# Both last down products at the end, residual sums in PSUM, and the down bias given once as gates times biases

## The reference

```python
logits = x @ w_router + b_router;  top_v, top_i = top_k(logits, 4);  gates = softmax(top_v)
gate = min(xb @ wg[e] + bg[e], 7);  up = clip(xb @ wu[e] + bu[e], -7, 7)      # 32 experts
y    = ((up + 1) * gate * sigmoid(1.702 * gate)) @ wd[e] + bd[e]
ffn  = sum over a token's 4 experts of its gate * y
out  = layernorm(2**0.25 * x + ffn + sigmoid(x @ w_ple_gate) * (p @ w_ple_proj))
```

## Time and profile before

| | us |
|---|---|
| three executions, median | 1250.95 (1250.07 to 1252.32) |
| profiled execution, its own time | 1253.7 |
| span of its profile | 1251.8 |
| PE busy / DVE / ACT / POOL | 1169.6 / 357.2 / 186.4 / 69.7 |
| moved | 442.18 MB, mean 353 GB/s |

### The profile page before, as it was taken

The page is one execution under the profiler, slowest core; times in us unless marked ns, Lnnn a source line. Parts: engine busy times, 40 slices in busy tenths (PEclk is TensorE's granted clock), DMA queues, the critical chain, the costliest instruction groups (busy, mean ns, idle before and its releaser), DMA issues.

```text
span 1251.8 us, 13175 instructions
## 1 busy us (share of the span) xinstructions
PE 1169.6 (93%) x5601; PEld 485.4 (39%) x5601; DVE 357.2 (29%) x568; ACT 186.4 (15%) x346; POOL 69.7 (6%) x74
## 2 busy tenths in 40 slices
PE   5999999899999997899999999999999999998985
PEld 4678775633333332243333333332323232322221
DVE  6866334531313130111222222122212121213014
ACT  2444342311001010020201000010101010110000
POOL 3100141110101030000000000000000000000000
PEclk9999999699999998999999999999999999999988
DMA  9652130689999999999999999999999999999892
GB/s 313 215 151 68 68 139 19 264 350 380 420 421 421 421 418 386 420 421 422 416 421 420 421 421 421 405 421 421 420 421 421 419 422 413 421 421 421 357 421 86
DMA packets 70509, 442.18 MB, mean 353 GB/s; under 512 B 7952, under 2 KB 8368, under 8 KB 21296
## 3 DMA queue, kind: packets, MB, share of 16 engines
q1 hardware_dynamic: 65600, 425.66, 83.5%
q0 software_dynamic: 4848, 15.64, 3.7%
HBM read 436.54 MB, written 4.73 MB: 353 GB/s over the span
## 4 chain that ended last, share of the span: by engine, by line
PE 73%; DMA 17%; DVE 7%; ACT 2%; issue 1%; SPq 1%; DVEq 0%
PE ps L1011 42%; DMA ring<-in_w_up 12%; PE ps L593 9%; PE ps L992 6%; DMA ring<-in_w_gate 4%; PE ps L944 3%; DVE y_s L1883 3%; PE ps L814 2%; DVE h_s L1881 2%; PE ps L999 2%; PE ps L621 1%; ACT hTe L1162 1%; PE ps L1027 1%; PE ps L976 1%; PE ps L948 1%
## 5 line engine op out<-in xcount | busy, mean ns | idle before, releaser
L1011 PE MATMUL ps<-ring,xTe 128*64 128x512 f32 x1536 | 358.1, 601 | 17.7 <-DMA ring<-in_w_up 14.5
L1011 PEld LDWEIGHTS ps<-ring,xTe 128*64 128x64 f32 x1536 | 105.5, 136 | 242.4 <-issue 242.2
L1011 PE MATMUL ps<-ring,hTe 128*64 128x512 f32 x768 | 180.8, 610 | 7.1 <-DMA ring<-in_w_down 7.1
L1863 DVE TENSOR_TENSOR xs<-xs,ps 128x512 f32<-128x512 f32 x64 | 44.0, 688 | 348.5 <-PE ps L992 348.4
L593 PE MATMUL ps<-xT,ring 128*128 128x288 f32 x448 | 115.4, 414 | 1.0 <-PE ps L593 0.6
L1011 PE MATMUL ps<-more,xTe 128*64 128x512 f32 x496 | 113.5, 599 | 1.6 <-DMA more<-in_w_up 0.8
L1011 PEld LDWEIGHTS ps<-ring,hTe 128*64 128x64 f32 x768 | 52.3, 139 | 121.8 <-issue 121.4
L593 PEld LDWEIGHTS ps<-xT,ring 128*128 128x128 f32 x448 | 84.8, 193 | 25.3 <-issue 2.3
L992 PE MATMUL ps<-y_s,GT 128*128 128x512 f32 (+1 forms) x256 | 82.5, 520 | 2.2 <-ACT y_s L1162 1.2
L1881 DVE TENSOR_SCALAR h_s<-ps 128x512 f32<-128x512 f32 x32 | 21.8, 681 | 161.0 <-PE ps L1011 161.0
L1162 ACT ACTIVATE h_s<-g_s 128x1024 f32<-128x1024 f32 x16 | 16.9, 1056 | 307.7 <-DVE g_s L1871 307.7
(11 more groups left out here) (371 smaller groups left out, 817.8 us busy)
## 6 DMA issues: line engine op xcount, KB each, us to landing
ring<-in_w_gate SPq DMA_DIRECT2D x96, 1024.0 KB, 11.2
ring<-in_w_up SPq DMA_DIRECT2D x96, 1024.0 KB, 11.7
ring<-in_w_down SPq DMA_DIRECT2D x96, 1024.0 KB, 13.6
more<-in_w_gate SPq DMA_DIRECT2D x32, 1024.0 KB, 9.9
more<-in_w_down SPq DMA_DIRECT2D x32, 1024.0 KB, 13.0
more<-in_w_up SPq DMA_DIRECT2D x30, 1024.0 KB, 13.1
ring<-in_w_in SPq DMA_DIRECT2D x28, 512.0 KB, 6.2
ring<-in_w_out SPq DMA_DIRECT2D x8, 512.0 KB, 5.1
```

What stands on the lines that cost most here:

```text
L1011: last = mm(ps[64 * q:64 * q + 64, bank0 + half, :], lhs(k, q), wide(t)[:, k % 2, half * 512:(half + 1) * 512], start=False, stop=k == KT - 1)
L1863: tt(x, x, ps[:, CB_BANKS[n], 0:512 if i < 2 else QW], ALU.add).then_inc(S["cb_added"], 1)
```

## The change

- **Order of the last stages.** gate and up of 14, gate and up of 15, down of 14, down of 15, for SP's loads and TensorE alike. h of 14 is transposed after step 1 of gate(15), h of 15 after step 3 of down(14) into a buffer of its own (`hTe_last`). Shares of pair 14 are made in down(15).
- **Sums in PSUM.** For the last two pairs the residual is brought into five banks by a matmul with the identity, the shares accumulate onto it there, and the statistics and the last norm read the banks. VectorE's adds for pairs 14 and 15 go. y of pair 15 is copied in two halves, by ScalarE and VectorE.
- **Down bias.** The bias matmuls of the down products and the preparation of the third bias vector go. All gates are transposed once, and each unit gets gates times b_down (fp32) in PSUM; b_down is loaded by POOL after the embedding weights.
- **Opening.** The wait for the key transposes moves to the last instruction of tile 1's norm; ScalarE's square root for it stands ahead of its key copies; `select` is split in `top_experts` and `chosen`, and the sample rows' norm comes before the subtractions; `prompt_states_b` runs before the sample rows' transposes; the first gather goes to banks 7 and 2, the gate product starts after the first copy; the second gather moves from up(0) to gate(0).

```diff
@@ tables
+SUM_BANKS = (6, 7, 0, 1, 4)
+LAST = NPAIR - 1
+STAGES = [(p, w) for p in range(NPAIR - 2) for w in range(3)] + \
+         [(LAST - 1, 0), (LAST - 1, 1), (LAST, 0), (LAST, 1), (LAST - 1, 2), (LAST, 2)]
@@ SP
-            for p in range(NPAIR):
-                for t, (w, k, q) in enumerate((w, k, q) for w in range(3) for k in range(KT // 2) for q in range(2)):
-                    t += p * PER
+            for stage, (p, w) in enumerate(STAGES):
+                for t, (k, q) in enumerate((k, q) for k in range(KT // 2) for q in range(2)):
+                    t += stage * KT
@@ POOL
-                for n, name in enumerate(("b_gate", "b_up", "b_down")):
+                for n, name in enumerate(("b_gate", "b_up")):
...
+            pool.wait_ge(S["ple_mm"], 5 * (KT + 1))
+            pool.dma_start(ple_w[0][0:NE, :], a["b_down"][0]).then_inc(S["ple_w_in0"], 16)
@@ TensorE
             row_stats(2)
+            prompt_states_b()
             transpose_normed(2)
...
             sample_ranks()
-            prompt_states_b()
             prompt_states_a()
...
+            def whole_unit(n, whole):
+                return mm(summed(n), ident, unit_of(n), start=True, stop=whole)
+            def all_gates():
+                for i, (t0, r) in enumerate(TILES):
+                    last = nc.tensor.transpose(ps[0:NE, 6, t0:t0 + r], gate_of[0:r, i, 0:NE], ident[0:r, 0:r])
+            def whole_with_bias(n):
+                whole_unit(n, False)
+                i, halves = (n // 2, (n % 2,)) if n < 4 else (2, (0, 1))
+                t0, r = TILES[i]
+                for half in halves:
+                    for out, c in columns(i, half, SUM_BANKS[n]):
+                        mm(out, GT[1][0:NE, t0:t0 + r], ple_w[0][0:NE, c], start=False, stop=False)
+            def last_h(k):
+                if k == 3:
+                    for half in range(2):
+                        h_transposes(LAST, half, half)
+                if k == 5:
+                    pe.wait_ge(S["hTe_ok"], 2 * LAST + 2)
+                if k in (5, 6):
+                    whole_with_bias(k - 3)
@@ products
-                for half in range(2):
+                for half in range(2 if w < 2 else 0):
@@ beside_gate
+                    if k in (1, 3):
+                        if k == 1:
+                            pe.wait_ge(S["OH_ok"], 1)
+                            pe.wait_ge(S["st_ok"], 2)
+                        gather(xTe[0], 2 * (k - 1), 4, 4 + k // 2, 128, 128)
+                    if k == 3:
+                        pe.wait_ge(S["xTe_ok"], 2)
...
+                elif p == LAST:
+                    if k == 1:
+                        for half in range(2):
+                            h_transposes(LAST - 1, half, 4 + half)
+                    if k == 3:
+                        pe.wait_ge(S["cb_added"], 5 * (LAST - 1))
+                        pe.wait_ge(S["ple_added"], 5 * (KT + 1))
+                        all_gates()
@@ beside_up
+                if p == LAST and k in (3, 4):
+                    if k == 3:
+                        pe.wait_ge(S["GT_ok"], NPAIR + 1)
+                        pe.wait_ge(S["ple_w_in0"], 16 * 6)
+                        pe.wait_ge(S["sel_ok"], NPAIR)
+                    whole_with_bias(k - 3)
@@ pairs
-                gather(xTe[0], 4 * n, 4, n, 0, 128)
+                gather(xTe[0], 4 * n, 4, ROW_BANKS[n], 0, 128)
-                pe.wait_ge(S["xTe_ok"], (2, 4)[p] if p < 2 else 4 + 8 * (p // 2))
+                pe.wait_ge(S["xTe_ok"], (1, 4)[p] if p < 2 else 4 + 8 * (p // 2))
...
+            def beside_last_down(k):
+                if 1 <= k <= 5:
+                    if k == 1:
+                        pe.wait_ge(S["y_ok"], LAST)
+                        whole_with_bias(4)
+                    combine_unit(k - 1, GT[(LAST - 1) % 3], SUM_BANKS[k - 1], False, False)
...
+            pe.wait_ge(S["y_ok"], NPAIR + 1)
             for n in range(5):
-                if n >= 2:
-                    pe.wait_ge(S["cb_added"], 5 * (NPAIR - 1) + n - 1)
-                combine_unit(n, GT[(NPAIR - 1) % 3])
+                combine_unit(n, GT[LAST % 3], SUM_BANKS[n], False)
@@ ScalarE
+            copy_y(LAST - 1)
+            act.wait_ge(S["cb_mm"], 5 * LAST)
+            act.wait_ge(S["y_mm"], 4 * LAST + 2)
+            f(y_s[:, 0:512], ps[:, 2, :], ACT.Copy).then_inc(S["y_ok"], 1)
@@ VectorE
+                    if n == 5:
+                        dve.wait_ge(S["kbt_mm"], 1)
...
-            dve.wait_ge(S["kbt_mm"], 1)
             norm(1, 5)
...
-            select(0)
+            top_experts(0)
             mixer_residual(2)
             tile_stats(2)
             spread_stats()
-            rest_of(1, 0)
+            chosen(0)
             norm_stats(2, 6)
             norm_apply(2, 6)
+            rest_of(1, 0)
+            rest_of(2, 0)
             rest_of(1, 1)
...
+            dve.wait_ge(S["cb_mm"], 5 * LAST)
+            dve.wait_ge(S["y_mm"], 4 * LAST + 4)
+            nc.vector.tensor_copy(y_s[:, 512:D], ps[:, 3, :]).then_inc(S["y_ok"], 1)
+            for n in range(5):
+                dve.wait_ge(S["cb_mm"], 5 * NPAIR + n - 4)
+                step(summed_stats(n))
```

More of the change, by code:

```diff
@@ L990, in combine_unit, with products @@
                 for half in halves:
[L991 to L992 removed]
+                    for out, c in columns(i, half, SUM_BANKS[n]):
[8 more added lines that the diff above has]
+                    whole_with_bias(k - 3)
+            def combine_unit(n, gt, bank=None, first=True, last_one=True):
+                bank = CB_BANKS[n] if bank is None else bank
+                i, halves = (n // 2, (n % 2,)) if n < 4 else (2, (0, 1))
+                t0, r = TILES[i]
+                for half in halves:
+                    for out, c in columns(i, half, bank):
+                        last = mm(out, gt[:, t0:t0 + r], y_s[:, c], start=first, stop=last_one)
                 last.then_inc(S["cb_mm"], 1)
[L995 to L998 removed]
+            def products(p, bank0, lhs, w, sel_p, after_k, done):
+                for half in range(2 if w < 2 else 0):
                     mm(ps[:, bank0 + half, :], sel_p[:, :, :].rearrange("p q s -> p (q s)"),
@@ L1001, in products @@
                 for k in range(KT):
-                    tiles = [(p if isinstance(p, int) else NPAIR) * PER + first + 2 * (k // 2) + q for q in range(2)]
+                    first = STAGES.index((p, w)) * KT if isinstance(p, int) else NPAIR * PER + w * KT
+                    tiles = [first + 2 * (k // 2) + q for q in range(2)]
                     if k % 2 == 0:
@@ L1011, in products @@
                             last = mm(ps[64 * q:64 * q + 64, bank0 + half, :], lhs(k, q),
-                                      wide(t)[:, k % 2, half * 512:(half + 1) * 512], start=False, stop=k == KT - 1)
+                                      wide(t)[:, k % 2, half * 512:(half + 1) * 512],
+                                      start=w == 2 and k == 0, stop=k == KT - 1)
                             if k == KT - 1:
@@ L1392, in _ @@
                             f(ple[:, i, 0:w], ple[:, i, 0:w], ACT.Sigmoid).then_inc(S["ple_sig"], 1)
-                else:
+                elif p == 0:
+                    for n in range(2):
+                        copy_rows(2 + n, xTe[0][:, 4 * n:4 * n + 4, 128:256], ps[:, 4 + n, :])
                     for n in range(2):
@@ L1396, in _ @@
                 swish(p)
-                if p == 0:
-                    for n in range(2):
-                        copy_rows(2 + n, xTe[0][:, 4 * n:4 * n + 4, 128:256], ps[:, 4 + n, :])
                 for n in range(4):
@@ L1444, in tile_stats @@
                     last = nc.vector.bn_stats(lns[:, i, q, :], x[:, q * 512:(q + 1) * 512] if i < 2 else x)
-                    (done or step)(last)
+                    step(last)
             def spread_stats():
@@ L2014, in _ @@
                         add_shares(j + NPAIR)
-                dve.wait_ge(S["cb_added"], extra * 5 + 5 * NPAIR)
-                for i in range(3):
-                    tile_stats(i, lambda last: last.then_inc(S["stats_anew"], 1))
+                for n in range(5):
+                    dve.wait_ge(S["out_mm"], 6 + n + 1)
+                    summed_stats(n).then_inc(S["stats_anew"], 1)
                 dve.wait_ge(S["stats_anew"], 5)
```

111 lines of the change are left out of this document (65 added, 46 removed).

## The result

The changed kernel takes 1245.13 us, median of eight executions (1241.68 to 1248.36); the kernel before, run beside it on the same chip, 1252.7 (1250.07 to 1254.13). The profiled execution took 1248.36, its span is 1246.5; it is 5.3 shorter than the span of before and the slowest of the eight.

The account below looks back on a forecast made before the run. The expert stage was taken as bound by the weight stream at about 421 GB/s. Terms 7.5 + 0.6 + 4.9 + 3.05 = 16.05 us, from the median 1250.95, gave 1235 us, range 1229 to 1243.

Parts of the forecast that it names:

- Order of the last stages: Pairs 14 and 15: TensorE goes straight from up(14) to gate(15) and ends 4.9 us earlier.
- 4.8 us loss of the stream: Weight stream near pair 14: 4.8 us lost while down(14) waited for h, to be recovered by the new order.
- TensorE's end: Last two pairs: gate(15) ends at 1167.2, up(15) 1185.6, down(14) 1207.2, down(15) 1226.6, 4.9 us earlier than 1231.5.
- rival 3: TensorE, not the stream, bounds the end, putting it back 2 to 4 us: 1237 to 1239; chance 0.12.
- Opening: Before pair 0: earlier norms, state products off the path and no copy wait bring 7.5 us in all.
- bound on both sides: TensorE's clock in the opening: gain 4.2 us if it returns no earlier, 12 if it never falls.
- rival 4: Stream takes nothing of the opening's gain, lost in a longer stand in pair 0: 1243; chance 0.06.
- Rival 1: Full clock in the opening: 4.5 us more gain, 1230.5; chance 0.15.
- rival 2: Opening gives little, by low-clock gathers or a ScalarE wait: gain 4.2 or less, 1238 to 1240; chance 0.17.
- Rival 5: Slower: opening keeps TensorE at 1.2 GHz through the gathers and into pair 0: 1256; chance 0.02.
- After the last product: From TensorE's end to the statistics' spread: gain 3.05 us; from spread to end unchanged at 11.2 us.
- Down bias: Removing thirty-two bias matmuls: nothing in the bound middle, 0.6 us in pair 0; VectorE's third bias vector: nothing.

Follow-up runs that it names:

- two pairs of runs: The changed kernel and the one with pair 15's selector made before h of pair 14, each run twice: 1245.13 and 1245.35 against 1242.5 and 1240.8 us.
- selector-early: Changed kernel with pair 15's selector made on VectorE before h of pair 14: 1242.5 and 1240.8 us, ratios 0.9915 and 0.9894 to the kernel before.
- fillers: selector-early plus eight 256-column matmuls in the opening whose result nobody reads: 1240.12 us, ratio 0.9903 to the kernel before.
- states in gate(0): selector-early with fillers and the mLSTM state products moved behind step 1 of gate(0): 1241.1 us, ratio 0.9906 to the kernel before.
- selector in the middle: Changed kernel with pair 15's selector made between h of pair 14 and the embedding adds: 1242.03 us, ratio 0.9917 to the kernel before.
- changed again: The changed kernel run a second time, unaltered: 1245.35 us, ratio 0.9935 to the kernel before.

## Why the prediction was wrong, point by point

**Order of the last stages: the step that failed.** I wrote that "after up(14) TensorE goes straight to gate(15)". I had followed h, the tiles and the transposes to their new places, but not the other operand of the product that was moved forward: its selector, made by VectorE at the end of pair 14. No list of waits of before could show this wait, since down(14) covered it; the program could, and so could VectorE's timeline, where `sel` starts at 1156.49, 5.5 us behind the end of up(14). The stand measured 5.87 us. Priced by the two pairs of runs, it cost 4.6 to 4.9 us at the end, and it kept the 4.8 us loss of the stream that I had counted as recovered: by the two stretches from 1140 it was 5.8 us. With the selector early 0.7 is left of it. The prediction's own sign, no stand over 1 us between up(14) and gate(15), failed; the wait that it named as a sign of being wrong, between gate(15) and up(15), stands one product later and did not come.

**TensorE's end: mis-sized by 3.2 us.** With the wait away, level to copy is 117.5, and I had 114.4. Measured from the end of up(14), selector-early takes 16.2 us for gate(15), as forecast; 20.6 for up(15) where I had 18.4, since two waits for tiles of 1.47 in all came already there, the units cost 2.1 each in place of 1.9, and the eight steps 14.4 in place of 14.0; 21.4 for down(14) (21.6); and 20.6 for down(15) in place of 19.4 (steps 14.7, shares 4.8 in place of 4.4, unit 4 1.2 in place of 1.0). This is rival 3, at 0.12: the stream ends at about 1211.7, counted from the 144 GB/s between 1210 and 1215, and TensorE at 1221.4. So recovering the stream's loss was worth less than its 4.8 us. (The formula of the prediction puts the last pair of down(15) at 1221.2 and not at 1219.5; TensorE was to need it only at 1223.1, so nothing hangs on it.)

**Opening: 5.2 in the first profile, 7.5 forecast.** Piece by piece, in the profile of after: the first router product starts 3.8 us earlier, where 3.1 was forecast; from there to the gathers it is 2.7 shorter, where 3.7 was forecast, with a wait of 1.15 for ScalarE's copy of the transposed rows that before did not have; and from the first gather to the first expert product it is 1.3 longer, where 0.7 less was forecast, since the gathers ran at half clock. So the steps went where the terms say, but the sum hung on the clock, which I had as a bound on both sides (4.2 and 12). Over the seven profiles whose opening is that of the change, the start lies between 237.86 and 243.62; the earliest has 6.8 us at half clock, the three latest 17.1. The forecast sits inside that scatter, so where a single profile falls in it is luck. Counted from the key transposes, the scatter goes with the length of the half clock: 25.2 us with 6.8 us at half clock, 26.7 with 10.2 (three profiles), 29.7 to 29.9 with 17.1 (three); before had 34.8, with 20.5. The rest of the scatter, 212.66 to 215.29 for those transposes, is older than the opening. The shift of the start reached pair 14 in full (863.1 to 864.1 from start to level in every kernel without work put into gate(0)), so rival 4 fell. Rival 1 (a start at 236.3) was not reached: the nearest was 237.86, and with fillers, where the clock did stay full, 238.4 (237.63 with the states in gate(0) too). The profile of after lies between the forecast and rival 2. Rival 5, slower by the clock, had the half clock under the gathers as it said, but not beyond 242.4, before pair 0.

**After the last product: right.** Forecast 3.05, measured 3.2; the rest 11.1. The Trainium skill ("VectorE: DVE Perf Modes", the TRN2 errata section) gives a PSUM source 62 cycles more; the trace does not agree here: statistics 0.70 from PSUM beside 0.71 from SBUF, and the first norm step of the two token tiles takes 1.22 and 1.28 us in both kernels, from SBUF before and from PSUM after:

```profile
1241.69 1.22 DVE L1468 SCALAR_TENSOR_TENSOR xs<-xs,mv,ln_g 128x1024 f32<-128x1024 f32 x1
```

```profile
1236.38 1.22 DVE L1560 SCALAR_TENSOR_TENSOR xs<-ps,mv,ln_g 128x1024 f32<-128x1024 f32 x1
```

**Down bias: right in kind.** 0.6 forecast and 0.6 measured from start to level with the bias alone left out; but kernels without these matmuls scatter from 863.1 to 864.1 there, the changed one's own profile has 864.0, and the 0.6 is no more than that scatter. The preparation that went from VectorE shows no gain: the key transposes start at 213.53 in before and 213.34 in after.

**The sum.** 16.05 were forecast and 5.3 came in the profiles: 2.3 short in the opening, 0.6 in the middle, 8.1 between level and copy (4.9 for the wait, 3.2 for the mis-sized end), less 0.25 better at the tail. In the medians 7.6 came; the profiled execution of after lies 3.2 above its median, that of before 1.0 above.

The best of the kernels with the whole result are the changed one with the selector made early (0.9915 and 0.9894 of the time before, in two jobs), the one with the selector in the middle (0.9917), and the early one with fillers (0.9903); these runs don't separate them.

## What to carry to other kernels

When a product is moved forward, list every operand and semaphore that its first instruction waits for, and find each one's producer in the order of its own engine's program; what a moved stage covered is in no list of waits, but the producer's own row has its time. A cheap producer (0.29 us here) at the back of a queue costs what stands ahead of it, and stands of 2.88 and 5.87 us on TensorE came here with a half clock behind them. Where a stretch hangs on the clock, forecast it as a spread and compare kernels by stretches, not by one total.

## What the runs showed of the hardware

- The same opening, instruction for instruction, started pair 0 anywhere from 237.86 to 243.16 us in five profiles of three kernels that differ only near the end (changed, changed again, selector early twice, selector between): the half clock began at 225.4, 227.3, 226.2, 228.2 and 227.7 and lasted 17.1, 10.2, 10.2, 10.2 and 6.8 us. Up to 2.6 us of the difference is older than the opening.
- TensorE can be busy in every microsecond of 17 and stay at half clock: the stretch 225.5 to 242.6 of after has 17.10 busy at 0.51. Its work there is products of 32 columns, ranks, the mLSTM states (128 and 256 columns) and gathers, and it had waited 1.15 us ahead of it. With matmuls of 256 columns in between, and that wait filled, the same products kept the full clock.
- The 5.87 us stand and the 2.88 us stand came with the same 6.8 us of half clock; waits of 1.31 us for tiles, in the kernel with the selector early, came with none.
